# The second expert table in blocks of 1 MB through three slots, and a decode ring of two rows

## The reference

```python
sc = jnp.einsum('nhpc,pkc->nhpk', q, sub_keys)          # 8 heads, 2 halves, 128 sub-keys
s_top, i_top = lax.top_k(sc, PEER_TOPK)                 # 16 per half -> 256 candidates -> 16
...
experts = (e1 * N_SUBKEYS + e2).reshape(N, 8 * 16)      # 128 experts of 16384 for each token
gates = jax.nn.softmax(c_top, axis=-1).reshape(N, 8 * 16)
u = u_tab[et]                                           # rows of the first table, 2048 wide
h = jnp.einsum('nd,nkd->nk', xt, u)
a = gt * jax.nn.gelu(h, approximate=False)
y = jnp.einsum('nk,nkd->nd', a, v_tab[et])              # rows of the second table
```

## Time and profile before

| | |
|---|---|
| median of three runs | 2531.74 us |
| the profiled execution | 2534.31 us |
| its span | 2532.5 us |
| first instruction on the second table's pieces to last matmul on them | 1628 to 2377 us |
| busy share of the span: PE, DVE, ACT, POOL | 70%, 70%, 35%, 45% |
| mean share of the 16 DMA engines busy, 1660 to 1956 us | 0.99 |

### The profile page before, as it was taken

One profiled execution on the slowest core, in us unless ns is written; L12 is line 12 of the kernel. 1 busy time (PEld: TensorE's weight loads), 2 busy tenths in 40 slices (PEclk: granted clock), 3 DMA queues, 4 the chain that ended last, 5 costly groups with the idle time before them and its releaser, 6 DMA issues.

```text
span 2532.5 us, 24956 instructions
## 1 busy us (share of the span) xinstructions
PE 1760.8 (70%) x9462; PEld 1439.9 (57%) x9462; DVE 1762.5 (70%) x2424; ACT 877.8 (35%) x1369; POOL 1140.5 (45%) x484
## 2 busy tenths in 40 slices
PE   7997899899969630000130222799999999999798
PEld 6875778787769510000030222677777777777676
DVE  1066232422147799999999998798988899987714
ACT  3223122223222110000290794644444444444332
POOL 3662233335636266688777885022222222221154
PEclk9998899999979765555555555899999999999899
DMA  9997999987999398899999998299999899998547
GB/s 355 382 377 269 378 412 399 403 350 290 377 333 356 124 402 348 349 422 422 421 401 385 422 422 333 89 384 385 388 380 381 319 373 384 382 382 304 208 182 257
DMA packets 131558, 881.86 MB, mean 348 GB/s; under 512 B 18962, under 2 KB 20562, under 8 KB 55540
## 3 DMA queue, kind: packets, MB, share of 16 engines
q1 hardware_dynamic: 76148, 477.65, 49.3%
q0 software_dynamic: 55296, 402.68, 39.5%
HBM read 871.28 MB, written 141.63 MB: 400 GB/s over the span
## 4 chain that ended last, share of the span: by engine, by line
PE 37%; DVE 25%; POOL 14%; DMA 10%; issue 10%; ACT 2%; SPq 0%; POOLq 0%; ACTq 0%; DVEq 0%
POOL expert_rows L535 11%; PE psum L1427 10%; PE psum L1429 10%; PE psum L1428 10%; DVE expert_rows L1243 9%; DMA v_raw<-in_peer_v 7%; DVE v_lo L1369 2%; POOL w_lo L521 2%; DVE expert_rows L1304 2%; DMA cache_part<-in_k_parts 2%; DMA expert_rows<-in_peer_u,experts 2%; PE psum L1586 1%; DVE x_tokens L1313 1%; PE psum L1442 1%; PE psum L1443 1%
## 5 line engine op out<-in xcount | busy, mean ns | idle before, releaser
L535 POOL DMA_INDIRECT expert_rows<-in_peer_u,experts x256 | 515.9, 2015 | 187.8 <-DVE expert_rows L1243 81.4
L1243 DVE SCALAR_TENSOR_TENSOR expert_rows<-expert_rows,x_tokens 128x2048 f32<-128x2048 f32 x256 | 577.9, 2288 | 31.8 <-DMA expert_rows<-in_peer_u,experts 30.8
L521 POOL TENSOR_TENSOR w_lo<-w_raw,w_hi 128x2048 fp32r<-128x2048 f32 x80 | 371.2, 4640 | 476.8 <-ACT w_hi L566 476.7
L1427 PE MATMUL psum<-v_hi,gate_matrix_hi 128*128 128x512 f32 x1024 | 405.4, 396 | 33.7 <-DVE v_lo L1369 33.3
L809 ACT ACTIVATE v_hi<-v_raw 128x1024 fp32r<-128x1024 f32 x256 | 271.4, 1060 | 400.6 <-DMA v_raw<-in_peer_v 299.2
L1429 PE MATMUL psum<-v_hi,gate_matrix_lo 128*128 128x512 f32 x1024 | 399.8, 390 | 0.0
L1428 PE MATMUL psum<-v_lo,gate_matrix_hi 128*128 128x512 f32 x1024 | 399.7, 390 | 0.0
L1369 DVE TENSOR_TENSOR v_lo<-v_raw,v_hi 128x1024 fp32r<-128x1024 f32 x256 | 310.1, 1220 | 77.9 <-ACT v_hi L809 77.5
L566 ACT ACTIVATE w_hi<-w_raw 128x2048 fp32r<-128x2048 f32 x80 | 153.1, 1914 | 364.6 <-PE psum L1429 273.8
L1427 PEld LDWEIGHTS psum<-v_hi,gate_matrix_hi 128*128 128x128 f32 x1024 | 192.5, 188 | 97.6 <-issue 35.6
L1706 PE MATMUL psum<-one_hot_first_gated,one_hot_second 128*128 128x128 f32 x384 | 88.1, 405 | 221.5 <-ACT one_hot_first_gated L739 210.3
(11 more groups left out here) (307 smaller groups left out, 3071.3 us busy)
## 6 DMA issues: line engine op xcount, KB each, us to landing
v_raw<-in_peer_v SPq DMA_DIRECT2D x256, 512.0 KB, 7.2
out<-in_state_attn_k SPq DMA_DIRECT2D x64, 1020.0 KB, 10.7
out<-in_state_attn_v SPq DMA_DIRECT2D x64, 1020.0 KB, 11.2
w_raw<-in_w_in SPq DMA_DIRECT2D x48, 1024.0 KB, 8.6
cache_part<-in_k_parts SPq DMA_DIRECT2D x40, 1024.0 KB, 9.9
cache_part<-in_v_parts SPq DMA_DIRECT2D x40, 1024.0 KB, 12.5
w_raw<-in_w_out SPq DMA_DIRECT2D x16, 1024.0 KB, 7.0
w_raw<-in_peer_wq SPq DMA_DIRECT2D x16, 1024.0 KB, 6.5
```

What stands on the lines that cost most here:

```text
L521: nc.gpsimd.tensor_tensor(l_, r_, h_.bitcast(f32), ALU.subtract).then_inc(w_lo_ready, 1)
L535: pool.indirect_dma_start(ring[n % NSLOT][:, :], None, u_tab, bass.IndirectOffsetOnAxis(idx_p[:, n // PAIRS, n % PAIRS:n % PAIRS + 1], 0)) ...
L1243: V.scalar_tensor_tensor(out=g, in0=g, scalar=1.0, in1=xt[:, t, :], op0=ALU.mult, op1=ALU.mult, accum_out=hdot[:, t, j:j + 1]).then_inc(u_ ...
L1427: MM(out, lh, rh, start=start, stop=False)
```

## The change

Five things are changed together.

- **Blocks instead of pieces in the loads.** SP loads a whole block k (128 rows of 2048 columns, 1 MB) with one DMA, 128 DMAs instead of 256. There are VP = 3 slots of 8 KB (24 KB instead of 20 KB) at 136, 144 and 168 KB. The load of block k waits until PE has used both pieces of block k - 3. The pieces themselves, and the work of ACT, DVE and PE on them, stay as they were: a piece is now half of a slot.
- **The first three loads** come in the order 0, 2, 1. Block 2 waits for the last prompt row (`u_free`, because its slot is the third slot of the prompt ring), block 1 for the last use of the tokens in its slot (`x_acc`, third count).
- **Four high parts** instead of three (HS = 4, at 176 to 192 KB). ACT may be four pieces ahead of PE.
- **The decode ring has two rows** instead of three (DSLOT = 2, at 152 to 168 KB). Gather i waits until DVE is done with row i - 2. The prompt ring keeps its seven slots at the same places (USLOT = 3 for the three that lie at 152 KB).
- **The bias of the second layer norm** lies where block slot 2 is, so its load is moved behind the last block load and waits until PE has used piece 251 (`vd_used` 252); gain and fold stay behind block 121 (pieces 242 and 243). `finish(0)` of the decode tokens is moved behind the last piece on DVE.

```diff
--- before.py
+++ after.py
@@ -37,13 +37,14 @@
 Z0 = 2 + TP
 IN_CHUNKS = (0, 1, 2, 3, 4, 5, 6, 7, 10, 11, 8, 9)
 NSLOT = 7
-DSLOT = 3
+DSLOT, USLOT = 2, 3
 PAIRS = PH * TOPK
 HALF = D // 2
 EG = 4
 GROUPS = 2 * 128 // EG
 PIECES = 2 * NK
-RL, HS, ST = 5, 3, 3
+RL, HS, ST = 6, 4, 3
+VP = RL // 2
 
 
 T_ALL = [(t, g, (4 * t + g) % 8) for t in range(3) for g in range(4)]
@@ -143,15 +144,16 @@
     dec = at("decode_T", [128, KT, 2 * TS], f32r, 108 * KB)
     thi = at("act_T_hi", [128, KT, N], f32r, 152 * KB)
     tlo = at("act_T_lo", [128, KT, N], f32r, 172 * KB)
-    ring = [at(f"expert_rows{i}", [128, D], f32, (152 if i < DSLOT else 96 - 24) * KB + i * 8 * KB) for i in range(NSLOT)]
+    ring = [at(f"expert_rows{i}", [128, D], f32, (152 if i < USLOT else 96 - 24) * KB + i * 8 * KB) for i in range(NSLOT)]
     xd2 = at("decode_out_tokens", [128, D], f32, 152 * KB)
     xt2 = at("prompt_out_tokens", [128, 2, D], f32, 0)
     emov = at("one_hot_first_gated", [128, 2, EG, NK], f32, 176 * KB)
     esta = at("one_hot_second", [128, 2, EG, NK], f32, 180 * KB)
-    V_AT = (136, 140, 148, 176, 144)
-    vrl = [at(f"v_raw{i}", [128, HALF], f32, a * KB) for i, a in enumerate(V_AT)]
-    vlo = [at(f"v_lo{i}", [128, HALF], f32r, a * KB) for i, a in enumerate(V_AT)]
-    vhi = [at(f"v_hi{i}", [128, HALF], f32r, (180 + 4 * i) * KB) for i in range(HS)]
+    V_AT = (136, 144, 168)
+    vrow = [at(f"v_rows{i}", [128, D], f32, a * KB) for i, a in enumerate(V_AT)]
+    vrl = [vrow[i // 2][:, (i % 2) * HALF:(i % 2 + 1) * HALF] for i in range(RL)]
+    vlo = [at(f"v_lo{i}", [128, HALF], f32r, (V_AT[i // 2] + 4 * (i % 2)) * KB) for i in range(RL)]
+    vhi = [at(f"v_hi{i}", [128, HALF], f32r, (176 + 4 * i) * KB) for i in range(HS)]
     S0 = 184 * KB
     top = at("top_values", [128, NF, TOPK], f32, S0)
     topi = at("top_keys", [128, NF, TOPK], u32, S0 + 1 * KB)
@@ -280,7 +282,7 @@
         act_step = sem("act_step")
         x_sc, x_acc = sem("x_scaled"), sem("x_in_sums")
         ple_out, ple_back = sem("ple_written"), sem("ple_read_back")
-        v_raw = [sem(f"v_slot{i}_in") for i in range(RL)]
+        v_raw = [sem(f"v_rows{i}_in") for i in range(VP)]
         ah_ok, al_ok, vh_ok = sem("gate_hi_ready"), sem("gate_lo_ready"), sem("v_hi_ready")
         vl_d, vd_used = sem("v_lo_dve"), sem("v_piece_used")
         y_rd = sem("prompt_sums_read")
@@ -476,24 +478,23 @@
             sp.dma_start(yp_v, ples[:, 1:3, :]).then_inc(ple_out, 16)
             sp.dma_start(ys_v, ples[0:TS, 0, :]).then_inc(ple_out, 16)
 
-            v_rows = v_tab.rearrange("(k p) (h c) -> p k h c", p=128, h=2)
-            for m in range(PIECES):
-                if m == 0:
+            v_rows = v_tab.rearrange("(k p) d -> p k d", p=128)
+            for k in (0, 2, 1, *range(3, NK)):
+                if k == 0:
                     sp.wait_ge(x_acc, 1)
-                if m == 2:
-                    sp.wait_ge(x_acc, 2)
-                if m == 3:
-                    sp.wait_ge(ab_mm, GROUPS)
-                if m == 4:
+                if k == 2:
+                    sp.wait_ge(u_free, 2 * PAIRS)
+                if k == 1:
                     sp.wait_ge(x_acc, 3)
-                if m >= RL:
-                    sp.wait_ge(vd_used, m - RL + 1)
-                sp.dma_start(vrl[m % RL][:, :], v_rows[:, m // 2, m % 2, :]).then_inc(v_raw[m % RL], 16)
-                if m == FOLD_AT:
+                if k >= VP:
+                    sp.wait_ge(vd_used, 2 * (k - VP) + 2)
+                sp.dma_start(vrow[k % VP][:, :], v_rows[:, k, :]).then_inc(v_raw[k % VP], 16)
+                if k == FOLD_AT // 2:
                     sp.wait_ge(d_free, 128)
                     sp.dma_start(xd2[0:TS, :], ydec[TS:128, :]).then_inc(fold_in, 16)
                     sp.dma_start(ln2[:, 0, :], ln2_g.rearrange("a d -> (a d)").partition_broadcast(128)).then_inc(ln2_in, 16)
-                    sp.dma_start(ln2[:, 1, :], ln2_b.rearrange("a d -> (a d)").partition_broadcast(128)).then_inc(ln2_in, 16)
+            sp.wait_ge(vd_used, PIECES - 4)
+            sp.dma_start(ln2[:, 1, :], ln2_b.rearrange("a d -> (a d)").partition_broadcast(128)).then_inc(ln2_in, 16)
 
             sp.wait_ge(al_ok, NK)
             for k in range(2):
@@ -803,7 +804,7 @@
                     A(ghs[:, k % ST, :], gm[:, :, k], ACT.Copy).then_inc(ah_ok, 1)
                 if m >= HS:
                     act.wait_ge(vd_used, m - HS + 1)
-                act.wait_ge(v_raw[m % RL], 16 * (m // RL + 1))
+                act.wait_ge(v_raw[k % VP], 16 * (k // VP + 1))
                 if m == 0:
                     act.wait_ge(u_free, 2 * PAIRS)
                 A(vhi[m % HS][:, :], vrl[m % RL][:, :], ACT.Copy).then_inc(vh_ok, 1)
@@ -1353,12 +1354,12 @@
                 V.memset(mx[:, 2:3], 0.0).then_inc(xd_ok, 1)
 
             def decode_centre():
-                dve.wait_ge(ln2_in, 32)
+                dve.wait_ge(ln2_in, 16)
                 centre(3, 0, (xd2[0:TS, :],))
 
             decode_parts = [xd2[0:TS, c * CW:(c + 1) * CW] for c in range(4)]
             decode_norm = {243: decode_sums, 245: lambda: moments(0, decode_parts), 247: lambda: variance(0),
-                           251: decode_centre, 253: lambda: finish(0)}
+                           251: decode_centre}
 
             for m in range(PIECES):
                 k = m // 2
@@ -1373,6 +1374,8 @@
                 if m in decode_norm:
                     decode_norm[m]()
 
+            dve.wait_ge(ln2_in, 32)
+            finish(0)
             dve.wait_ge(vd_used, PIECES)
             sums = [[PS[:, b, :] for b in OUT_BANKS[t]] for t in range(2)]
             moments(1, sums[0])
```

## The result

The changed kernel takes 2563.05 us (median of four runs, 2562.62 to 2568.45) where the kernel before takes 2532.19 (four runs, 2524.23 to 2537.15): a ratio of 1.0115, 95% interval 1.0096 to 1.0134. It is slower by 31 us; 2567 was forecast.

The account below looks back on a forecast made before the run. PE, DVE and DMA were nearly equally loaded; the two-row decode ring would decide. 27 + 11 + 2 - 5 = +35 us on the profiled 2534.3 gave 2569; that execution lay 2.6 above the median, so 2567, range 2515 to 2616.

Parts of the forecast that it names:

- The ring's term: Decode ring of two rows: DVE waits for gathered rows, +27 us in the first half and +11 in the second.
- L: Time from a decode gather's issue to its landing, put at 8.5 us; each 0.5 us is worth 31 us.
- The reason for L = 8.5: Median of six gathers at the stage's start, engines 0.93 busy; a slower pace was to unload them about as much.
- "I count nothing" for the table's loads: Second table's loads: 24 KB lead in coarser steps counted at nothing, since the wait for decode rows covers it.
- Longer L from larger rows: Rival at the decode gathers: 8 KB table rows push them back, L 9.2, +79 us, 2611; chance 0.16.
- Transfers of 1 MiB: Table loads: by the skill's formula 4.4 us for one of 1 MB against 6.4 for two; not counted.
- ACT's wait for pieces: Sign in the changed profile: ACT's wait for table pieces from HBM should shrink from 299.2 us.
- if ACT's wait for blocks grows instead, it is the three slots: Sign in the changed profile: growth of ACT's wait would point to the table's three block slots.
- The three block slots: Rival at the table's slots: released in steps of two pieces, 6.2 us per block, +48 us, 2577; chance 0.13.
- Start and end: Stage's start: third gather later, +2 us once; stage's end: bias moved and block 121 early, 5 us saved.

Follow-up runs that it names:

- six pieces: Table loads of 512 KB through six slots, late bias: 2492.4 us with decode ring of three and three high parts; 2585.2 us as changed kernel with ring of two.
- The run with three high parts: The changed kernel with three high parts instead of four (HS = 3): 2563.7 us.
- the late bias alone: The kernel before with only the bias load behind the last piece and `finish(0)` behind the loop: 2529.9 us, ratio 0.9986.
- blocks by columns: The changed kernel with each block loaded by two DMAs of 1024 columns (4 KB per partition, 512 KB): 2579.6 us.
- ring of two alone: The kernel before with only the decode ring cut from three rows to two: 2601.6 us, ratio 1.027.
- loads of 64 partitions: The changed kernel with each block loaded by two DMAs of 64 partitions (8 KB per partition, 512 KB): 2872.8 us.

## Why the prediction was right, and where not

The forecast of 2567 us lies 4 us from the median, and its main mechanism is shown: the ring of two makes DVE wait for gathers, and everything behind DVE with it. Taking one row of the ring away from the kernel before costs 68 us, giving it back to the changed kernel gains 32.

- **The ring's term.** 27 + 11 us were given, 22 + 12 measured. The rows start 5.45 and 5.59 us apart where 5.53 and 5.57 were said. L was put at 8.5 and its median is 8.2. But this L is no single number: the gathers in the chain from 1660 to 1956 us take 7.2 to 11.6 us, and the shortest of all takes 5.5. DVE waits for 60 rows, not for all; the median in the ring's sum comes near the mean pace (5.38 against 5.45 us in the first half), not that of each row.
- **The reason for L = 8.5 was only half right.** I took it from a lighter load, and the load did get lighter (a share of 0.95, where 0.93 was said). At the same lighter load, with the table's pieces as they were, L is 8.8 and the whole is 38 us slower than the changed kernel. What made up for it are parts that I had counted at nothing or at little: the sixth slot, the fourth high part and the late bias (16 us together, with the ring of two) and the blocks (22, about 15 of them by rows of 8 KB). The number is right partly by luck, because two errors cancel: the ring alone costs more than my term, and the blocks, under this ring, gain.
- **"I count nothing" for the table's loads** was the step that failed, though it did not spoil the number. The argument was that DMA engines 0.99 busy leave no gain in the lead, and that the wait for rows covers the rest. The six pieces with three rows show 400 GB/s and a stage at PE's limit. The kernel before was held by how far ahead the table was asked for.
- **Longer L from larger rows**, the rival that the Trainium skill's rule on turns between queues suggested (DMA: Bandwidth & Descriptors, Queues, rings and completion order), did not come: L is 8.2 with 8 KB rows in one DMA, 8.3 with 4 KB rows in one, 8.8 with pieces.
- **Transfers of 1 MiB.** The Trainium skill's advice (DMA: Bandwidth & Descriptors, section Bandwidth) is not borne out as such: with three rows, 512 KB in six slots beat 1 MB in three by 39 us; with two rows it was the other way round, by 22. The 2.0 us that the prediction put beside the advice stand in the Trainium skill, same page, section Anatomy of one DMA, for DMAs that GpSimd issues, where these loads are SP's.
- **ACT's wait for pieces** was to shrink from 299.2 us and grew to 407.8. The run with three high parts explains it. ACT's waits for pieces and for PE together went from 400 to 437 us. The sign "if ACT's wait for blocks grows instead, it is the three slots" was badly chosen: it came, and the ring was the main cause.
- **The three block slots** as the cause of the loss: fallen as the main cause, since with three rows the blocks take 2531. That they cost 39 us against six pieces is real, but hidden behind a gain of equal size from 4 KB more.
- **Start and end.** +2 was given for the third gather, and DVE waited 0.3 us for it. The -1.1 at the start lies ahead of this stage: the last prompt row starts at 1563.8 before and at 1562.6 after. For the fold -5 was given; the stretch that holds it is 3.9 us shorter, and the pause between the halves 1.3, but the late bias alone is not clear of noise. `finish(0)` waited 1.4 us for the bias and was done before PE, as said.

What stays open: why gathers land sooner beside loads that come by blocks (8.2 and 8.3 against 8.8), and why rows of 8 KB shorten the wait for high parts. Whether six pieces and blocks by columns differ at all under the ring of two is not shown: their 6 us (1.5 by the ratios) are within their intervals.

## What to carry to other kernels

A ring of n slots gives one item every (use + issue + landing) / n, and the landing time to put in is that of the loaded queues; compare the result with the pace before taking a slot away, even where nobody waits for the ring. DMA engines shown 0.99 busy need not be at their limit: if transfers are late, try one more slot in the buffer they land in before making them larger. With a ring long enough, the same memory was worth 39 us more in fine pieces, each released and landing by itself; with the ring too short, the large blocks were the better by 22. Try both where the neighbour's ring is short. And add up the waits of the engine whose list paces the stage: a change can move a wait from one cause to another.

## What the runs showed of the hardware

- A busy share of 0.99 went with 383 GB/s, and one of 1.00 with 400, for the same mix of 4 KB and 8 KB rows. With loads of 64 partitions a share of 0.98 went with 253 GB/s. The share says that packets are in flight, not how fast they go.
- A load of 64 partitions x 8 KB beside gathers is much slower than one of 128 partitions x 4 KB: the two forms have the same bytes (512 KB), and the whole kernel took 2872.8 against 2579.6 us.
- The time from issue to landing of a 1 MB gather depends on the load, but the busy share does not give it: median 6.2 us at a share of 0.62, 8.2 at 0.95 beside blocks, 8.8 at 0.93 beside pieces (ring of two alone), 9.0 at 0.99, and 14.0 at 0.98 beside the loads of 64 partitions.
- Rows of 8 KB instead of 4 KB in the table's loads did not make the gathers beside them land later: median 8.2 against 8.3 us, each with one DMA of 1 MB per block.
